# A three-branch mixer before a mixture of experts: the last branch as product, gate, gate, an output projection that opens on two panels, and a gate product ahead of a norm

## What is computed

```python
h = rms_norm_2(x, norm_mix[l]) * (1.0 + scale_m) + shift_m
proj = h @ w_in[l]
m_z, m_xbc, m_dt, sb_qkv, g_qkv, g_a, g_b, g_gate, br_gate = jnp.split(proj, split_points, axis=-1)
y_a = mamba2_branch(...)           # branch 0
y_b = stick_breaking_branch(...)   # branch 1
y_c = gated_deltanet_branch(...)   # branch 2
branch_proj = jnp.einsum("bsie,ied->bsid", branches, w_branch[l])     # 3 x (512 -> 1024)
gates = jax.nn.sigmoid(br_gate)                                       # 3 x 1024, from h
merged = jnp.sum(gates * branch_proj, axis=2)
x = x + gate_m * (merged @ w_out[l])
h = rms_norm_2(x, norm_ffn[l]) * (1.0 + scale_f) + shift_f
y = hier_moe(h, ...)               # 32 experts, top 2 of one group
x = x + gate_f * y
```

## Time and profile before

| what | value |
|---|---|
| median of three runs | 1608.63 us (1608.3 to 1609.04) |
| the profiled execution's own time | 1611.41 us |
| its span, first to last instruction | 1609.6 us |
| mean granted TensorE clock over the span | 0.96 of full speed |
| busy share of the span: PE, PEld, DVE, ACT, POOL | 93%, 78%, 48%, 35%, 18% |
| last branch: its first panel starts, its last panel ends | 1041.04 us, 1078.6 us |
| output projection: first matmul, last residual | 1085.97 us, 1113.57 us |

### The profile page before, as it was taken

How to read it: one execution, slowest core, us unless ns; L and a number is a source line. 1 busy time by engine, 2 the same in 40 slices (tenths; PEclk the granted TensorE clock), 3 DMA queues, 4 the chain that set the end, 5 groups by cost and what they waited for, 6 DMA issues and landing times.

```text
span 1609.6 us, 28268 instructions
## 1 busy us (share of the span) xinstructions
PE 1499.6 (93%) x11238; PEld 1252.1 (78%) x11238; DVE 780.5 (48%) x1411; ACT 571.4 (35%) x895; POOL 294.6 (18%) x121
## 2 busy tenths in 40 slices
PE   7978999999999999999998988978799999999897
PEld 5857999999868999989997977978566665555554
DVE  4963888648674888434543524552422222111212
ACT  2245545454345555356553115433111111101101
POOL 0021112212201212227760002672000000000000
PEclk9989999999999999989999987998899999999999
DMA  7674555664434555625541212463899999999995
GB/s 289 235 275 146 168 169 169 195 235 153 137 134 134 182 185 180 199 92 163 172 144 40 66 40 77 168 239 129 327 424 425 427 428 430 426 427 427 428 427 227
DMA packets 64609, 375.82 MB, mean 233 GB/s; under 512 B 7296, under 2 KB 7552, under 8 KB 49152
## 3 DMA queue, kind: packets, MB, share of 16 engines
q1 hardware_dynamic: 64512, 374.43, 61.9%
HBM read 373.35 MB, written 1.05 MB: 233 GB/s over the span
## 4 chain that ended last, share of the span: by engine, by line
PE 62%; issue 13%; DMA 11%; DVE 8%; SPq 2%; ACT 2%; POOL 1%; POOLq 0%; DVEq 0%; ACTq 0%
PE lin L673 8%; PE lin L675 8%; PE lin L674 8%; DMA modrow<-in_experts 7%; PE mixp L1292 4%; PE mixp L1296 4%; PE stat L1317 4%; DVE mixers L1933 3%; PE lin L692 2%; DMA moe_low<-in_experts 2%; DMA moe_high<-in_experts 2%; DVE cat L2117 1%; PE stat L1260 1%; PE stat L673 1%; PE mixp L673 1%
## 5 line engine op out<-in xcount | busy, mean ns | idle before, releaser
L673 PE MATMUL lin<-r_hi,w_hi 128*128 128x256 f32 x1464 | 428.7, 293 | 14.9 <-POOL w_lo L1737 5.1
L674 PE MATMUL lin<-r_lo,w_hi 128*128 128x256 f32 x1464 | 418.5, 286 | 0.0
L675 PE MATMUL lin<-r_hi,w_lo 128*128 128x256 f32 x1464 | 418.4, 286 | 0.0
L673 PEld LDWEIGHTS lin<-r_hi,w_hi 128*128 128x128 f32 x1464 | 285.4, 195 | 23.0 <-POOL w_lo L1737 6.7
L674 PEld LDWEIGHTS lin<-r_lo,w_hi 128*128 128x128 f32 x1464 | 285.6, 195 | 0.9
L675 PEld LDWEIGHTS lin<-r_hi,w_lo 128*128 128x128 f32 x1464 | 285.2, 195 | 0.0
L1741 POOL TENSOR_TENSOR w_lo<-ring,w_hi 128x1024 fp32r<-128x1024 f32 x71 | 175.4, 2483 | 236.2 <-ACT w_hi L1358 235.8
L1770 DVE TENSOR_TENSOR w_lo<-ring,w_hi 128x1024 fp32r<-128x1024 f32 x126 | 156.5, 1246 | 85.3 <-ACT w_hi L1364 65.2
L1737 POOL TENSOR_TENSOR w_lo<-ring,w_hi 128x1024 fp32r<-128x1024 f32 x42 | 108.3, 2578 | 481.7 <-ACT w_hi L1364 298.4
L1364 ACT ACTIVATE w_hi<-ring 128x1024 fp32r<-128x1024 f32 x124 | 129.6, 1048 | 57.4 <-PE mixp L675 48.5
L1358 ACT ACTIVATE w_hi<-ring 128x1024 fp32r<-128x1024 f32 x119 | 124.0, 1049 | 35.4 <-PE lin L675 17.4
(11 more groups left out here) (460 smaller groups left out, 2834.0 us busy)
## 6 DMA issues: line engine op xcount, KB each, us to landing
ring<-in_panels SPq DMA_DIRECT2D x272, 512.0 KB, 3.6
moe_high<-in_experts SPq DMA_DIRECT2D x32, 2048.0 KB, 30.0
moe_low<-in_experts SPq DMA_DIRECT2D x32, 2048.0 KB, 30.1
aring<-in_ada SPq DMA_DIRECT2D x24, 1024.0 KB, 6.1
ring<-in_experts SPq DMA_DIRECT2D x10, 2048.0 KB, 27.7
cst<-in_experts SPq DMA_DIRECT2D x10, 1280.0 KB, 28.3
sq<-in_experts SPq DMA_DIRECT2D x10, 1024.0 KB, 28.9
rs<-in_experts SPq DMA_DIRECT2D x10, 512.0 KB, 30.1
```

Source lines behind the costliest of these rows:

```text
L673: pe.matmul(o, w_hi[:, slot, c], r[0], start=start, stop=False, skip_group_check=True)
L674: pe.matmul(o, w_hi[:, slot, c], r[1], start=False, stop=False, skip_group_check=True)
L675: return pe.matmul(o, w_lo[:, slot, c], r[0], start=False, stop=stop, skip_group_check=True)
```

## The change

Three things move; no arithmetic is added or dropped.

1. **Branch 1 in the order product, gate, gate.** `is_gate` gives branches 0 and 1 that order and branch 2 the old one; the host lays out branch 1's panels accordingly. TensorE waits for y1's split rows ahead of panel 0 of the branch. ScalarE's roundings of `merged` move between the gates, VectorE's `gate_branch` steps through banks as in branch 0.
2. **The output projection opens with two panels interleaved over k**: for each k, the three matmuls of panel 0, then the three of panel 1. The other six follow as before.
3. **`gate_branch(0, 3)` goes ahead of the DeltaNet norm** on VectorE. On ScalarE the upper part of panel 2 of branch 2 (`BRANCHES2 + 1`) goes behind the last two tanh of branch 0.

```diff
         def is_gate(i, j):
-            return j % 3 != 0 if i == BRANCHES[0] else j < KD
+            return j < KD if i == 2 else j % 3 != 0
...
             def project(rows, first=False):
 
-                for m in range(KD):
+                if first:
+                    opening = [split_panel(j) for j in range(2)]
+                    for b in opening:
+                        bank(b)
+                    for i in range(KD):
+                        pe.wait_ge(h_ready, seen(h_ready))
+                        for b in opening:
+                            mm = split_matmul(lin[b][:, 0:T], (b, slice(i * P, (i + 1) * P)), [t[:, i, :] for t in rows],
+                                              i == 0, i == KD - 1)
+                            if i == KD - 1:
+                                mm.then_inc(panel_done, 1)
+                    panels.advance(2)
+                for m in range(2 if first else 0, KD):
                     b = split_panel()
                     bank(b)
-                    split_linear(b, first and m == 0, rows)
+                    split_linear(b, False, rows)
...
-                    if split and (i, j) in ((2, 1), (2, KD), (1, KD)):
+                    if split and (i, j) in ((2, 1), (2, KD), (1, 0)):
                         pe.wait_ge(h_ready, seen(h_ready, KD if j == 1 else 1))
...
             next_split[0] = BRANCHES2
-            split_hi(BRANCHES2 + 2)
+            split_hi(BRANCHES2 + 1)
             gates(0, 10, 12)
             split_hi(BRANCHES2 + 3)
...
             gates(2, 8, 12)
-            gates(1, 0, 10)
-            round_merged(0, 2)
-            gates(1, 10, 11)
-            round_merged(1, 2)
-            gates(1, 11, 12)
-            round_merged(2, 2)
-            round_merged(3, 1)
+            gates(1, 0, 6)
+            round_merged(0, 6)
+            gates(1, 6, 9)
+            round_merged(1, 6)
+            gates(1, 9, 12)
+            round_merged(2, 6)
+            round_merged(3, 3)
...
             def gate_branch(i, pair):
 
-                first = i == BRANCHES[0]
-                if not first and pair == 0:
+                in_turn = i != 2
+                if not in_turn and pair == 0:
                     panels.advance(KD)
...
-                    panels.taken(1 + m if first else u - KD - pair)
+                    panels.taken(1 + m if in_turn else u - KD - pair)
...
-                panels.advance(3 if first else 1)
+                panels.advance(3 if in_turn else 1)
...
                 dve.tensor_copy(b_vt[:, c, :], mixbank(c)).then_inc(ev("b_vt_copied"), 1)
+            gate_branch(0, 3)
             dve.wait_ge(ev("g_o_read"), 1)
...
             dve.tensor_tensor(ybr[:, 8:12, :], ybr[:, 8:12, :], gg, ALU.mult).then_inc(ev("yc_done"), 1)
-            gate_branch(0, 3)
             dve.wait_ge(ev("b_l_ready"), 1)
...
-        if i == 0:
+        if i != 2:
             stream.append(_np.concatenate([branch, own.reshape(4, 2, P, D)], axis=1).reshape(12, P, D))
```

More of the change, by code:

```diff
@@ L1586, in gates @@
                     if is_gate(i, j):
-                        u = 2 * (j // 3) + j % 3 - 1 if i == BRANCHES[0] else j
+                        u = j if i == 2 else 2 * (j // 3) + j % 3 - 1
                         b = panels.done()
```

## The result

The changed kernel takes 1594.72 us, the median of six runs (1588.88 to 1601.48), against 1608.84 us for the kernel before, also six runs (1606.37 to 1610.95): a ratio of 0.9921, 95% interval 0.9892 to 0.9951, or 8 to 17 us less. The profiled execution took 1591.19 us with a span of 1589.3 us and a mean granted clock of 0.972 (before: 1611.41, 1609.6 and 0.960).

What follows compares the result with a forecast made beforehand. It took the serial path ahead of the expert loop, whose weight stream sets the pace to the end, as the bound; -0.9 + 5.3 + 1.45 = 5.85 us off the 1608.63 us median gave 1602.8 us, range 1598.0 to 1606.0.

Steps and rivals of the forecast that it cites:

- Part 1: Gated product 0.9 ahead of the DeltaNet norm: a loss of 0.9 us taken, with +3.0 us as the other end.
- The row that the forecast leaned on: Second FFN: GpSimd's 2.66 us operation went ahead of two VectorE subtractions, which took 4.57 us for some 2.4 us of work.
- 1.6 us of low clock: Attention products behind the masks: TensorE's wait of 3.4 us was expected to lower the clock, costing 1.6 us.
- Part 2: Branch 1 as product, gate, gate: the projection starts at 1080.65, not 1085.97 us, a gain of 5.3 us.
- Part 3: Output projection opened with two interleaved panels: 26.1 us instead of 27.6, a gain of 1.45 us.
- Sum: The three parts together, -0.9 + 5.3 + 1.45 = 5.85 us off the total.
- VectorE keeps the port: Rival at the second mask: VectorE goes ahead of GpSimd, 9.75 us gained in all, 1598.9 us; chance 0.28.
- The range: Total time from 1598.0 to 1606.0 us, taking in the forecast, the port rival and a cold projection opening.
- the routing's clock: Routing behind the projection runs partly at the lower clock; 1 us or so was allowed for it.
- 3.2 us for what a measurement can tell: Whole kernel: about 0.2% (3.2 us) was taken as what a measurement can tell from no change.

Runs made afterwards that it cites:

- e6: Changed kernel with ScalarE's upper part of panel 2.5 made earlier, so GpSimd asks for the port ahead of VectorE's masks; profiled span 1604.1 us.
- e7: Changed kernel with ScalarE's upper part of the projection's panel 3 made ahead of the first square, not behind it; profiled span 1602.6 us.
- e5: Changed kernel with the output projection's first two panels run singly again, not interleaved; profiled span 1591.5 us.
- e10: Changed kernel with ScalarE's upper part of panel 2.5 one tanh later, so GpSimd starts after VectorE's second mask; 1599.39 us, ratio 0.9940.
- e2: Changed kernel with gated product 0.9 back behind the norm, leaving the new branch order and projection opening; 1601.97 us, ratio 0.9968.

## Why the prediction was wrong, and where it was right

**Part 1 failed.** The step is: "GpSimd is ahead by less than 0.1 us; I take -0.9, because the row that it is nearest to has GpSimd winning." The schedule was right: product 0.9 over in time, no wait ahead of 2.1, GpSimd's row 0.01 to 0.02 us ahead of the second mask. But a row that starts ahead of another by that little doesn't say who gets the port. The row that the forecast leaned on was no such tie: there GpSimd began at 645.42 us and the two subtractions that waited for it at 645.73, 0.31 us apart. VectorE got it five times in six, and part 1 gives 3.1 to 3.4 us, the upper end. The rule that the forecast named (the Trainium skill, SBUF — State Buffer, Who interferes with whom: who issues first holds the port for a whole instruction) agrees with e6, where each mask stood still for a whole operation of GpSimd; for the near tie no run here shows who issued first. The price was wrong as well: the forecast added 1.6 us of low clock to a late mask, and behind the late mask of e7 the clock stayed up. Even with GpSimd ahead, part 1 gains about 1 us (14.2 to 14.4 against 13.22).

**Part 2 was right.** C to P fell by 5.14 us, 5.3 forecast. The projection starts 1.66 us behind 1.11 (1.6 forecast), 1.4 waited 0.36 us (0.6), and nothing waited for y1.

**Part 3 was right but for its size:** 1.12 us, 1.45 forecast. The clock stayed up, and panel 3 waited 0.78 us (0.95). The missing 0.3 us lie between the start of panel 3, at 1078.94, and its residual, at 1082.12: 3.2 us, where the forecast had 2.88; the four panels behind it took 3.3 us each, as forecast. e5, which has the clock but not the interleaving, keeps 0.65 us of this gain (P to L 26.95, not 27.60).

**Sum.** 3.1 + 5.1 + 1.1 = 9.3 us: the rival "VectorE keeps the port", with 9.75 us and 1598.9 us, was the true case.

**The range failed too.** It allowed "1 us or so for the routing's clock" and nothing for the code ahead. In 14 traces the first Abs stood between 988.44 and 997.93 us, and routing varied by 2.4 us, both by the granted clock, with either kernel. The six runs of before first timed were all at 1606 us or above, where later ones reached down to 1596.64; the changed kernel's reached 1588.88. Of the 14 us between the first medians, 9.2 to 9.7 us are the change, and the rest is what six runs of each kernel happened to draw of this scatter: with 12 runs against 35 the ratio, 0.9946, makes 8.7 us. The forecast's 3.2 us for what a measurement can tell was too small too: its first interval, 8 to 17 us, is 9 us wide. What tips the clock at the program's start in one run and not in another, and how that carries to 850 us, was not tried and stays open.

## What to carry to other kernels

Measure a change between two marks of the trace that enclose it, the first ahead of all that it moves: here that gave 9.2 to 9.7 us from single traces, where six runs of a kernel left 8 to 17. Where two engines reach for a shared port within a few hundredths of a microsecond, price both outcomes, and don't choose by a row in which the lead was longer; or move one of them, as e10 did. A wait taken away is worth its length and what the clock loses behind it; a wait as long at another place may cost its length alone.

## What was not expected

A wait's length did not tell whether the clock would fall: 2.57 or 2.58 us ahead of 2.1 lowered it in all five traces of before and in e2, 3.08 us ahead of the attention products in e7 did not, 4.86 us at the same place in e6 did. And 0.01 to 0.02 us of lead in a row decided nothing about the port: 0.69 us for the mask in five traces, 2.88 in the sixth.
